# Sixteen of 48 modulation units computed on VectorE instead of TensorE, in a two-model transformer kernel

## What is computed

```python
mod = silu_c @ ada_w[layer] + ada_b[layer]
shift_m, scale_m, gate_m, shift_f, scale_f, gate_f = jnp.split(mod, 6, axis=-1)
h = modulate(rms_norm_2(x, norm_mix_w[layer]), shift_m, scale_m)     # h * (1 + scale) + shift
...
x = x + gate_m[:, None, :] * y
h = modulate(rms_norm_2(x, norm_ffn_w[layer]), shift_f, scale_f)
x = x + gate_f[:, None, :] * conv_ffn(h, ffn_w_up[layer], ffn_conv_w[layer], ffn_conv_b[layer], ffn_w_down[layer])
```

## Time and profile before

| | us |
|---|---|
| three runs | 1129.7, 1132.2, 1133.1 |
| median | 1132.2 |
| profiled execution | 1130.73 |
| its span, first to last instruction | 1129.0 |
| busy in the span: TensorE | 1077.7 |
| VectorE | 735.5 |
| ScalarE | 586.3 |
| GpSimd | 83.9 |

### The profile page before, as it was taken

One profiled execution on the slowest core, in us unless ns is written; L12 is line 12 of the kernel. 1 busy time (PEld: TensorE's weight loads), 2 busy tenths in 40 slices (PEclk: granted clock), 3 DMA queues, 4 the chain that ended last, 5 costly groups with the idle time before them and its releaser, 6 DMA issues.

```text
span 1129.0 us, 22056 instructions
## 1 busy us (share of the span) xinstructions
PE 1077.7 (95%) x9350; PEld 1010.7 (90%) x9350; DVE 735.5 (65%) x1095; ACT 586.3 (52%) x888; POOL 83.9 (7%) x93
## 2 busy tenths in 40 slices
PE   6999999999999989999898999999999989999997
PEld 6988778898989989989567899999989989999997
DVE  6467656654667686795775776774476766767643
ACT  5555654644455564632654755553454455556433
POOL 2000000100201361000111000000010010000000
PEclk9999999999999999999999999999999999999999
DMA  8556565786776585533676655455465567564631
GB/s 268 183 189 234 198 208 184 219 274 217 231 239 201 172 206 164 172 114 113 241 275 231 224 184 190 154 204 203 149 224 187 170 200 256 166 204 165 223 113 38
DMA packets 165774, 219.81 MB, mean 195 GB/s; under 512 B 4481, under 2 KB 146205, under 8 KB 165676
## 3 DMA queue, kind: packets, MB, share of 16 engines
q1 hardware_dynamic: 164442, 215.67, 58.2%
q0 software_dynamic: 832, 1.65, 0.7%
q10 hardware_dynamic: 402, 1.08, 0.4%
HBM read 217.27 MB, written 1.11 MB: 193 GB/s over the span
## 4 chain that ended last, share of the span: by engine, by line
PE 47%; DVE 5%; ACT 2%; DMA 1%; issue 1%; DVEq 0%; ACTq 0%
PE psG L491 11%; PE psG L493 10%; PE psG L492 10%; PE psS L493 4%; PE psS L491 4%; PE psS L492 4%; PE psG L592 1%; DVE wlo L1582 1%; ACT whi L1053 1%; PE psY L617 1%; DVE Hlo L1647 1%; DMA raw<-in_ev_w_out_dram 1%; DMA raw<-in_ffn_w_up_dram 1%; DVE vt L1638 0%; DVE stat L2042 0%
## 5 line engine op out<-in xcount | busy, mean ns | idle before, releaser
L1582 DVE TENSOR_TENSOR wlo<-raw,whi 128x1024 fp32r<-128x1024 f32 x311 | 376.2, 1245 | 155.4 <-ACT whi L1053 150.4
L491 PE MATMUL psG<-Hlo,whi 128*128 128x256 f32 x1520 | 436.8, 287 | 12.9 <-DVE wlo L1582 5.2
L493 PE MATMUL psG<-Hhi,whi 128*128 128x256 f32 x1520 | 429.3, 282 | 0.0
L492 PE MATMUL psG<-Hhi,wlo 128*128 128x256 f32 x1520 | 429.0, 282 | 0.0
L1053 ACT CAST whi<-raw 128x1024 fp32r<-128x1024 f32 x311 | 316.1, 1048 | 123.5 <-PE psS L493 68.3
L491 PEld LDWEIGHTS psG<-Hlo,whi 128*128 128x128 f32 x1520 | 287.6, 189 | 21.7 <-issue 10.5
L492 PEld LDWEIGHTS psG<-Hhi,wlo 128*128 128x128 f32 x1520 | 287.9, 189 | 0.1
L493 PEld LDWEIGHTS psG<-Hhi,whi 128*128 128x128 f32 x1520 | 287.4, 189 | 0.0
L491 PE MATMUL psS<-Glo,whi 128*128 128x256 f32 x352 | 99.5, 283 | 0.0
L492 PE MATMUL psS<-Ghi,wlo 128*128 128x256 f32 x352 | 99.1, 282 | 0.0
L493 PE MATMUL psS<-Ghi,whi 128*128 128x256 f32 x352 | 99.1, 282 | 0.0
(11 more groups left out here) (378 smaller groups left out, 1654.8 us busy)
## 6 DMA issues: line engine op xcount, KB each, us to landing
raw<-in_ada_w_dram SPq DMA_DIRECT2D x48, 1024.0 KB, 5.5
raw<-in_ffn_w_up_dram SPq DMA_DIRECT2D x44, 1024.0 KB, 5.1
raw<-in_w_in_dram SPq DMA_DIRECT2D x29, 1024.0 KB, 6.9
raw<-in_ev_w_in_dram SPq DMA_DIRECT2D x26, 1024.0 KB, 5.6
raw<-in_ffn_w_down_dram SPq DMA_DIRECT2D x22, 1024.0 KB, 4.8
raw<-in_od_w_in_dram SPq DMA_DIRECT2D x12, 1024.0 KB, 5.2
raw<-in_w_in_dram SPq DMA_DIRECT2D x9, 512.0 KB, 6.1
raw<-in_w_o_dram SPq DMA_DIRECT2D x4, 1024.0 KB, 7.9
```

The source lines that it names most:

```text
L491: mm(o, a_hi, b_lo, start=first, stop=False, skip_group_check=shared)
L492: mm(o, a_lo, b_hi, start=False, stop=False, skip_group_check=shared)
L493: return mm(o, a_hi, b_hi, start=False, stop=last, skip_group_check=shared)
L1582: V.tensor_tensor(ring_half(wlo, v, h - H0[v]), src, ring_half(whi, v, h - H0[v]).bitcast(F32), ALU.subtract).then_inc(lo_split, 1)
```

## The change

Four rows, 7, 8, 10 and 11, move to VectorE; a unit of these is of kind "G". It is loaded like the others, takes no bank, and `add_rows` multiplies each of its two 128x1024 halves with the silu of c (one number per partition) and adds it to `arow`. The first instruction of a row is a multiplication alone (L1692 of the changed kernel), the other seven multiply and add (L1694); each waits for the one before. When the four units of a row are in, TensorE spreads it (`spread`: four matmuls with the row's 256-column parts against ones, into four groups of 32 partitions of `psX`), ScalarE copies 256 columns back (`keep_spread`), and `sum_ada` and `keep_ada` go on as before. GpSimd folds only the eight rows left.

The places of all units are now a table. Rows 0 to 2 are computed in slots 0 to 11, rows 3 to 6 in the neighbourhood attention (sixteen units in the same places as before, with other contents), row 9 in the two tails ahead of the first feed-forward and the third block. None stand in slots 12 and 13, the merge gates, `wo`, ahead of the second feed-forward, or on TensorE in its up-projection. The VectorE units stand in the first up-projection behind iterations 0, 2, 4, 6, 8, 10, in the first down-projection behind 0, 2, 4, 6, 8, in the third block behind its first part, and in the second up-projection behind 1, 3, 5, 7. The sums of rows 3, 4 and 5 move to later places, and `ada_bank` alternates between two pieces of `psX`.

```diff
+ON_VECTOR = (7, 8, 10, 11)
+ADA_AT = {f"slot{i}": (i // 4, i % 4) for i in range(12)}
+ADA_AT.update({place: (3 + i // 4, i % 4) for i, place in enumerate(NA_PLACES)})
+ADA_AT.update({place: (7, i) for i, place in enumerate(("up0.0", "up0.2", "up0.4", "up0.6"))})
+ADA_AT.update({place: (8, i) for i, place in enumerate(("up0.8", "up0.10", "fd0.0", "fd0.2"))})
+ADA_AT.update({place: (9, i) for i, place in enumerate(("tail0a", "tail0b", "tail1a", "tail1b"))})
+ADA_AT.update({place: (10, i) for i, place in enumerate(("fd0.4", "fd0.6", "fd0.8", "od0"))})
+ADA_AT.update({place: (11, i) for i, place in enumerate(("up1.1", "up1.3", "up1.5", "up1.7"))})
...
-            if br != "c":
-                ada(f"gates{i}{br}", 1)
...
-        ada(f"wo{i}", int(i < 2))
...
-            ada(f"up{layer}.{i}", int(layer == 1 and i < 2))
+            ada(f"up{layer}.{i}")
...
-    banked = [int(k[0] != "D") for k in UNITS]
+    banked = [int(k[0] not in "DG") for k in UNITS]
...
-        ada_bank = psX[:, 0:2 * KT]
+        def ada_bank(n):
+            return psX[:, 16 * (n % 2):16 * (n % 2) + 16]
...
-        UP_SUMS = ({1: 6, 3: 7, 5: 8, 7: 9}, {3: 11})
+        UP_SUMS = ({1: 5, 3: 6, 9: 7}, {10: 11})
+        UP_SPREAD = ({8: 7}, {9: 11})
...
+                elif u >= RAW and UNITS[u - RAW][0] == "G":
+                    sp.wait_ge(row_added, ON_DVE.index(u - RAW) + 1)
...
+            def spread(n):
+                pe.wait_ge(row_added, ADDED[n])
+                pe.wait_ge(ada_kept, n)
+                for j in range(4):
+                    last = mm(psX[32 * j:32 * j + 32, 0:256], ones[:, 0:32], ada_row(n)[:, j * 256:(j + 1) * 256],
+                              start=True, stop=True)
+                last.then_inc(row_spread, 1)
...
-                    if br != "c":
-                        ada(f"gates{i}{br}")
-                if i == 0:
-                    sum_ada(3)
-                elif i == 1:
-                    pe.wait_ge(ada_kept, 4)
+                if i == 1:
+                    pe.wait_ge(pT_kept, NT0)
+                    pe.wait_ge(ada_kept, 3)
                     turn_tokens(1)
-                elif i == 2:
-                    pe.wait_ge(turned_kept, 8)
-                    sum_ada(4)
...
-                ada(f"wo{n}")
-            sum_ada(5)
...
             for n, u in enumerate(SPAN["evoA"]):
                 project(u, Hhi, Hlo)
-                if n:
+                if n == 0:
+                    pe.wait_ge(pT_kept, NT0 + 2 * NA)
+                    sum_ada(3)
+                    sum_ada(4)
+                else:
                     sum_part(F["ffn0"], n - 1)
...
-                    ada(f"up{layer}.{i}")
+                    if i in UP_SPREAD[layer]:
+                        spread(UP_SPREAD[layer][i])
...
+                        if layer == 0 and i == 4:
+                            spread(8)
+                        elif layer == 0 and i == 6:
+                            sum_ada(8)
...
+                    sum_ada(9)
+                elif i == 2:
+                    spread(10)
+                elif i == 3:
                     sum_ada(10)
...
+            def keep_spread(n):
+                act.wait_ge(row_spread, ADDED[n] // 4)
+                nc.scalar.copy(ada_row(n)[:, 0:256], psX[:, 0:256]).then_inc(row_ready, 1)
+                act.wait_ge(row_ready, n + 1)
...
+            def add_rows(place):
+                for u in SPAN[f"ada_{place}"]:
+                    n, q = ada_part(u)
+                    r = ada_row(n)
+                    w = raw[:, u % RAW, :].rearrange("p (k n) -> p k n", k=2)
+                    dve.wait_ge(raw_landed[u % RAW], LANDED[u])
+                    for k in range(2):
+                        c = cs[:, UNITS[u][2] + k, 0:1]
+                        if q == 0 and k == 0:
+                            ins = V.tensor_scalar(r, w[:, k, :], c, None, ALU.mult)
+                        else:
+                            ins = V.scalar_tensor_tensor(r, w[:, k, :], c, r, ALU.mult, ALU.add)
+                        if k == 0:
+                            step(ins)
+                    then(ins, row_added, ON_DVE.index(u) + 1)
...
                     if i in UP_SUMS[layer]:
                         keep_ada(UP_SUMS[layer][i] + 1)
+                    add_rows(f"up{layer}.{i}")
                 for i in range(FT // 2):
                     if i < FT // 2 - 1:
                         ahead(SPAN[f"fd{layer}.{i}"][0])
+                    add_rows(f"fd{layer}.{i}")
...
                 split_value(z, Ghi[:, 2 * i:2 * i + 2, :], Glo[:, 2 * i:2 * i + 2, :], G_ready, n + 1)
+                add_rows(f"od{i}")
...
-            for n in range(5):
+            for n in range(3):
                 fold_row(n)
```

More of the change, by code:

```diff
@@ L69, in section, with ada @@
             units.append((kind, src, k0, col0 + i * (width if step is None else step), width))
-    def ada(place, n):
-        spans[f"ada_{place}"] = list(range(len(units), len(units) + n))
-        for _ in range(n):
-            q = sum(unit[0] == "A" for unit in units)
-            units.append(("A", f"ada{q // 24}", q % 4 * 2, q // 4 % 6 * D, D))
+    def ada(place):
+        spans[f"ada_{place}"] = []
+        if place in ADA_AT:
+            n, q = ADA_AT[place]
+            spans[f"ada_{place}"].append(len(units))
+            units.append(("G" if n in ON_VECTOR else "A", f"ada{n // 6}", 2 * q, n % 6 * D, D))
     first = {"qa": ("F", O_QA), "ka": ("F", O_KA), "va": ("T", O_VA), "qb": ("B", O_QB), "kvb": ("M", O_KB),
@@ L89, in plan_units @@
             proj(name, i)
-        ada(f"slot{s}", 1)
+        ada(f"slot{s}")
     for i in range(4):
@@ L106, in plan_units @@
     for step in range(10):
-        ada(f"na{step}a", 1)
+        ada(f"na{step}a")
         if 5 <= step < 9:
             section(f"evoB{step - 5}", "U", "ev_w_outB", 256 * (step - 5), 1)
-        ada(f"na{step}b", int(step < 5 or step == 9))
+        ada(f"na{step}b")
     spans["evoB"] = [spans[f"evoB{n}"][0] for n in range(4)]
@@ L122, in ffn @@
             section(f"fv{layer}.{i}", "F", f"ffn_up{layer}", FF + i * 256, 1)
-            ada(f"up{layer}.{i}", int(layer == 1 and i < 2))
+            ada(f"up{layer}.{i}")
         for i in range(FT // 2):
             section(f"fd{layer}.{i}", "D", f"ffn_down{layer}", 0, 1, width=D, k0=2 * i)
+            ada(f"fd{layer}.{i}")
     ffn(0)
@@ L149, in build @@
            "ffn_down0": ffn_w_down_2[0], "ffn_down1": ffn_w_down_2[1], "ada0": ada_w_2[0], "ada1": ada_w_2[1]}
-    halves = {"C": 1, "U": 1, "V": 1, "A": 0}
+    halves = {"C": 1, "U": 1, "V": 1, "A": 0, "G": 0}
     NH = [halves.get(k[0], 2) for k in UNITS]
@@ L161, in build @@
     after = dict(zip(split_order, split_order[1:]))
-    ADA = [u for u in range(NU) if UNITS[u][0] == "A"]
+    ON_PE = [u for u in range(NU) if UNITS[u][0] == "A"]
+    ON_DVE = [u for u in range(NU) if UNITS[u][0] == "G"]
     with ExitStack() as ctx:
@@ L400, in build @@
         SLOT = [[SPAN[name][i] for name, i in units] for units in BESIDE]
-        KEEPS = [u for u in range(SLOT[-1][-1] + 1) if UNITS[u][0] not in "CA" and u not in
+        KEEPS = [u for u in range(SLOT[-1][-1] + 1) if UNITS[u][0] not in "CAG" and u not in
                  SPAN["ga"] + SPAN["gb"] + SPAN["gc"]]
@@ L406, in build @@
         EVO_AT = {5: 0, 6: 1, 7: 2, 8: 3}
-        UP_SUMS = ({1: 6, 3: 7, 5: 8, 7: 9}, {3: 11})
+        UP_SUMS = ({1: 5, 3: 6, 9: 7}, {10: 11})
+        UP_SPREAD = ({8: 7}, {9: 11})
+        FOLDS = [n for n in range(12) if n not in ON_VECTOR]
+        ADDED = {n: 4 * i + 4 for i, n in enumerate(ON_VECTOR)}
         KEPT = {name: KEEPS.index(SPAN[name][-1]) + 1 for name in ("ka", "va", "kvb", "kc", "vc")}
@@ L465, in _ @@
                                      ).then_inc(raw_landed[slot], 16)
-                elif kind in "DA":
+                elif kind in "DAG":
                     sp.dma_start(r.rearrange("p (k n) -> p k n", k=2),
@@ L603, in sum_ada @@
                 for c in range(2):
-                    last = mm(ada_bank[:, 8 * c:8 * c + 8], ada_row(n)[:, c * P:(c + 1) * P],
+                    last = mm(ada_bank(n)[:, 8 * c:8 * c + 8], ada_row(n)[:, c * P:(c + 1) * P],
                               sel8[:, :, :].rearrange("p q w -> p (q w)"), start=True, stop=True)
@@ L1071, in keep_rows @@
                 for u in SPAN[f"ada_{place}"]:
[L1072 to L1075 removed]
+                    n, q = ada_part(u)
+                    act.wait_ge(ada_done, ON_PE.index(u) + 1)
+                    if q == 0 and n == 2:
+                        act.wait_ge(row_summed, 1)
                     nc.scalar.copy(ada_row(n)[:, q * 256:(q + 1) * 256], bank(u)[:, 0:256]
@@ L1272, in _ @@
                         high_of(2)
-                    if br != "c":
-                        keep_rows(f"gates{i}{br}")
                 if i == 0:
@@ L1517, in feed_forward @@
                     act.wait_ge(gelu_out, FT // 2 * layer + i + 1)
-                    keep_rows(f"up{layer}.{i}")
```

(15 more changed lines are left out.)

47 lines of the change are left out of this document (25 added, 22 removed).

## The result

The changed kernel takes **1137.3 us** (median of ten runs, 1134.7 to 1140.5) against 1132.4 for the kernel before (ten runs beside it): ratio 1.0046, 95% interval 1.0029 to 1.0063. It is slower by some 5 us; forecast were 1125.3 and a range that ended at 1131. Its profiled execution took 1139.1 (span 1137.3), at the slow end of the ten.

A forecast was written before the change was run, and what follows sets the result against it. TensorE, busy 1077.7 of 1129.0 us, was taken as the bound. Removed work of 18.2 us, less 1.1 for sums, 2.8 for spreads and 8.1 for VectorE overruns, left 6.2 us less: 1125.3 us, range 1117.5 to 1131.

The forecast's parts named there:

- Removed in front (15.1): Slots 12 and 13, merge gates and output projection: units, sums and bank waits taken out save 15.1 us.
- the rival of lost gate time: Merge gates: freed time turns into waits, half of 15 us is lost, giving 1132; chance 0.14.
- Price of an addition (1.30): VectorE: each 128x1024 multiply-and-add takes about 1.30 us, two take 2.7.
- overrun (1.0 per iteration): Up-projections: a 2.7 us unit stands before the split and exceeds TensorE's slack by 1.0 us per iteration.
- spreads: TensorE: four spreads of 0.7 us each, 2.8 added in all (1.4 to 4.4).
- The second up-projection's first overrun (0.5): Second up-projection, iteration 1: the row's first, shorter unit of 2.1 us overruns by 0.5 us.
- The five units beside the down-projection cost nothing: First down-projection: split 2.4 and addition 2.7 fit in 5.7 us of TensorE per unit, so cost is nothing.
- loads hidden ... in the down-projection more: Loads queued behind VectorE's slot release stay hidden, over 3 us to spare in the up-projection, more in the down-projection.
- Third block (0.5 overrun): Third block: its one unit overruns by 0.5 us, as the product waits for the bank there as well.
- evoA: "its four small additions lie in a wait for GpSimd": Ahead of the first feed-forward: additions lie in a wait; only the two sums count, +0.7 us for the stretch.
- one fall, ahead of the second feed-forward: Clock rival: TensorE idles some 3 us there and its clock may fall, worth 0.3 to 1.5 us; chance 0.07.
- The slower rival: VectorE becomes the bound: additions at 2.60 us each overrun by 3.7 in ten places, about 1150; chance 0.07.

The follow-up runs named there:

- experiment 2: Changed kernel with VectorE's up-projection additions moved into the next iteration, behind the split of the fv weights: 1130.0 us (0.9977 to the kernel before).
- experiment 5: Changed kernel with the six down-projection and third-block units loaded, but one 8-column VectorE operation instead of two 1024-column ones: 1129.1 us.
- experiment 6: Changed kernel with those six units' slots freed after one 8-column operation, then two 1024-column operations on a spare row to keep VectorE's time: 1132.7 us.
- experiment 3: Changed kernel with ScalarE's last cast of each down-projection moved behind the table load and squares: 1132.9 us (0.9994 to the kernel before).
- experiment 7: Changed kernel with additions behind the split, ScalarE's last down-projection cast behind the squares, third block's unit moved to up-projection iteration 9: 1130.4 us (0.9992 to kernel before).
- experiment 8: Changed kernel with additions behind the split and twelve units in successive iterations, one per first up-projection iteration, one in the down-projection: 1160.5 us (1.0253 to kernel before).
- experiment 9: Changed kernel with the edits of experiment 2 and experiment 3, plus the third block's addition between first product and odc split: 1122.7 us (0.9912 to kernel before).
- experiment 12: experiment 9 plus four fillers of eight matmuls in TensorE's two waits ahead of the first feed-forward: 1121.8 us (0.9893 to the kernel before).

## Why the prediction was wrong, point by point

- **Removed in front (15.1): right in the sum**, 15.2 measured, bank waits included; the rival of lost gate time falls. Slots 12 and 13 gave 1.4 (forecast 1.7), the gates 9.4 (9.3), the output projection 4.35 (4.1); the last two are within 0.2 us of this in all eleven traces with this front and no fillers in the gates. Two misses cancel in the gates, though. Up to the wait for a split that ends at 217.8 they are 1.2 us longer, where 0.1 less was forecast; the rest gave 10.6 instead of 9.2. The lost part begins with a TensorE wait of 2.85 us (1.15 before) that the units taken out of the slots leave behind, and with a clock fall at 199.9; such a fall stands at 198 to 202 in every trace with this front and in neither of the kernel before. The part ahead of the gates moves with the clock as well: 2.9 to 3.2 us less than before in the six traces without a fall up to there, 0.9 to 1.5 in the four with one, as before has.
- **Price of an addition (1.30) and overrun (1.0 per iteration): right**, 1.3 and 0.96 to 1.09; spreads 0.66 net (0.7 forecast). The second up-projection's first overrun (0.5) did not come. That the addition stands ahead of the split, not in the 2.76 us behind it, is shown by experiment 2. The Trainium skill, "VectorE: DVE Perf Modes", section "The TRN2 errata", gives 58 cycles plus one per element, an estimate of 1.13; this trace does not agree.
- **"The five units beside the down-projection cost nothing", "loads hidden ... in the down-projection more": this step failed.** I checked VectorE's time against TensorE's there, and it has room. I did not follow the freed slot onwards: SyncE's in-order queue, a load used in the next stage, ScalarE's in-order queue, the squares. It cost 4.5 us (experiments 5 and 6), some 2.2 of them a clock fall behind the wait that it made; the late cast is the last link (experiment 3). Some 1 us more of that stretch stays without a cause. In the up-projection the claim held only as long as every second iteration has no unit: two in a row cost 6.7 us more, eleven 37, clock falls behind the waits included (experiments 7 and 8).
- **Third block (0.5 overrun): mis-sized.** I reckoned that the product's wait for the bank would take up most of it. The gap is 2.4, nearly the whole pair of additions; without it the block is 2.3 us shorter (experiments 5 and 9).
- **evoA: "its four small additions lie in a wait for GpSimd": the clock was not looked at.** 4.2 us instead of 0.7. About 3.0 of it are two falls of the granted clock; without them the stretch is at +1.2 (experiment 12), of which the sums were to be 0.7. The ten runs of the changed kernel have mean clocks of 0.983 to 0.990, the runs of the kernel before 0.991 to 1.000. I forecast one fall, ahead of the second feed-forward, where TensorE's wait is now 3.12 us and was 1.26. It came in all twelve traces with the change's front. The prediction took that from the Trainium skill, "TensorE: Matmul & The Clock Gate", section "Part 1: The HAM clock gate", which says that an idle TensorE falls to 1.2 GHz; it does not say that a wait as short as this one is followed by a fall each time. The window over it:

```profile
925.00:935.00 10.00, 6.81 (x39) 6.39 (x40) 8.78 (x18) 6.17 (x13) 0.00 (x0) 0.83 0.31 107
```

  against 1.00 before. I had the mechanism and priced it at one place only; the trace has six stretches of 3.4 us at 1.2 GHz more than the kernel before up to the last down-projection (at 200, 524 to 531, 592, 606, 818 and 930 us, where before has one at 548).
- **The slower rival** (VectorE at 2.60 an operation) was the wrong mechanism: the sign came out its way through a queue and the clock, not through a slow operation.

Together the three failed steps are 5.5 us (down-projection), 1.9 (third block) and 3.5 (evoA); 3.1 more lie between the front and evoA.

**Open:** the kernel before has the same TensorE wait of 2.27 us ahead of evoA, and 1.83 inside it where the changed kernel has 2.28, and no fall there in two traces; the eleven others without fillers at this place have one or two. Experiment 12 shows, with one trace, that filling the waits removes the falls, not why they began. The 3.1 us ahead of evoA (1.8 to 2.4 in the other traces of this front without fillers in the gates) have clock falls in them, 3.4 to 6.8 us at 1.2 GHz against 3.4 before, and were not taken apart.

## What to carry to other kernels

When work moves to an engine with free time, look at what its instructions hold, not only at how long they take: a buffer slot of a short ring, and behind it every load of an in-order queue, and behind a late load every instruction of the engine that casts it. Put the moved work behind the critical instruction of each period (here behind the split), never ahead of it: that alone was worth 7 us, 5.9 of it in the up-projections, and a wait filled exactly, as in the third block, another 2.3. And work taken off an engine leaves holes that may cost it its clock; compare the granted clock over all stages, not only at the place of the edit.

## What was not expected of the hardware

- Loads at 349 GB/s over 37 us of the down-projection (experiment 5; 200 in the kernel before) cost TensorE at most 0.6 us there.
- TensorE waits of 2.3 us were followed by 3.4 us at 1.2 GHz, 1.5 us lost each, and four groups of eight small matmuls in them kept the clock at 2.4 GHz. In the kernel before a wait of 2.27 and one of 1.83 at these places were not followed by one.
